# DeltaNet scan: a triangular inverse that begins in packed 32x32 blocks and is joined twice, with decay masks and output sums on other engines

## What is computed

```python
decay = exp(where(incl, g_cum[:, None] - g_cum[None, :], -inf))
a_mat = where(strict, (beta * k) @ k.T * decay, 0)
wu    = solve_triangular(a_mat + eye, [beta*k*exp(g_cum), v*beta])   # per chunk
qk    = (q @ k.T) * decay
# then, chunk after chunk, with the state S (64 x 64 per head):
v_new = u - w @ S
o     = (q * exp(g_cum)) @ S + qk @ v_new
S     = S * exp(g_last) + k_tail.T @ v_new
y     = o_forward + flip(o_backward)
```

## Time and profile before

| | |
|---|---|
| median of 3 runs | 4050.82 us (4047.32 to 4050.98) |
| profiled execution, its own time | 4048.99 us |
| its span | 4047.2 us |
| mean granted TensorE clock | 0.976 |
| TensorE busy | 3825.9 us, 95% |
| VectorE, ScalarE, POOL busy | 1951.6, 1121.1, 905.1 us |

### The profile page before, as it was taken

The page is one execution under the profiler, slowest core; times in us unless marked ns, Lnnn a source line. Parts: engine busy times, 40 slices in busy tenths (PEclk is TensorE's granted clock), DMA queues, the critical chain, the costliest instruction groups (busy, mean ns, idle before and its releaser), DMA issues.

```text
span 4047.2 us, 75588 instructions
## 1 busy us (share of the span) xinstructions
PE 3825.9 (95%) x32478; PEld 3201.9 (79%) x32478; DVE 1951.6 (48%) x3457; ACT 1121.1 (28%) x2430; POOL 905.1 (22%) x659
## 2 busy tenths in 40 slices
PE   6999999899899999999998999999899899999997
PEld 5668888788787888888886668878788778888886
DVE  3455566444456333333357464565444564333446
ACT  3444242333413111111114452252333321000111
POOL 1000100122103333333322001100222034443442
PEclk8999999899899999999998999999999899999999
DMA  4230000100000101101111120001000101111111
GB/s 179 102 149 32 22 22 22 61 3 3 23 32 32 42 31 41 42 31 41 41 40 73 63 105 22 22 12 42 32 3 3 43 32 53 42 52 52 41 52 52
DMA packets 30518, 180.81 MB, mean 45 GB/s; under 512 B 2592, under 2 KB 7968, under 8 KB 15136
## 3 DMA queue, kind: packets, MB, share of 16 engines
q1 hardware_dynamic: 28944, 173.66, 11.7%
q10 hardware_dynamic: 1296, 3.07, 0.2%
HBM read 168.32 MB, written 8.39 MB: 44 GB/s over the span
## 4 chain that ended last, share of the span: by engine, by line
PE 85%; DVE 8%; ACT 4%; issue 2%; DMA 1%; POOL 1%; ACTq 0%; POOLq 0%; DVEq 0%; SPq 0%
PE ps L1364 37%; PE ps L768 9%; PE ps L778 8%; PE ps L803 4%; PE ps L901 3%; PE ps L1228 3%; PE ps L1236 2%; PE ps L1239 2%; PE ps L943 2%; PE ps L986 1%; PE ps L1317 1%; PE ps L1207 1%; PE ps L812 1%; PE ps L1291 1%; PE ps L1008 1%
## 5 line engine op out<-in xcount | busy, mean ns | idle before, releaser
L1364 PE MATMUL ps<-Yn_parts,ring_parts 128*128 128x512 f32 (+1 forms) x3888 | 798.9, 367 | 2.4 <-DVE Yn_parts L2610 2.1
L1364 PEld LDWEIGHTS ps<-Yn_parts,ring_parts 128*128 128x128 f32 x3888 | 671.2, 189 | 126.7 <-DVE Yn_parts L2610 5.4
L1364 PE MATMUL ps<-temp_parts,ring_parts 128*128 128x512 f32 (+1 forms) x2560 | 726.5, 369 | 5.0 <-DVE Hn_parts L2551 3.6
L2871 POOL TENSOR_TENSOR ring_parts<-ring,consts 128x2048 fp32r<-128x2048 f32 x62 | 286.5, 4621 | 1187.4 <-DMA ring<-in_ff 1187.4
L1364 PEld LDWEIGHTS ps<-temp_parts,ring_parts 128*128 128x128 f32 x2560 | 464.9, 189 | 88.0 <-DVE Hn_parts L2551 4.1
L768 PE MATMUL ps<-ring_parts,Xn_parts 128*128 128x256 f32 x2560 | 506.1, 293 | 24.1 <-DVE Hn_parts L2122 16.2
L2498 DVE SCALAR_TENSOR_TENSOR Xn<-ps,mods,Xn 128x256 f32<-128x256 f32 (+1 forms) x364 | 251.7, 692 | 574.2 <-PE ps L1364 504.3
L1364 PE MATMUL ps<-Hn_parts,ring_parts 128*128 128x512 f32 (+1 forms) x1280 | 471.4, 368 | 0.0
L768 PEld LDWEIGHTS ps<-ring_parts,Xn_parts 128*128 128x128 f32 x2560 | 418.4, 196 | 27.3 <-issue 22.6
L1926 ACT ACTIVATE Yn<-ps 128x256 f32<-128x256 f32 (+1 forms) x160 | 88.6, 554 | 1237.6 <-PE ps L1364 1237.6
L2609 DVE TENSOR_TENSOR Yn<-Yn 128x256 f32<-128x256 f32 (+1 forms) x160 | 191.3, 1196 | 402.7 <-ACT Yn_parts L1928 402.7
(11 more groups left out here) (318 smaller groups left out, 5610.1 us busy)
## 6 DMA issues: line engine op xcount, KB each, us to landing
ring<-in_ff SPq DMA_DIRECT2D x64, 1024.0 KB, 4.7
ring<-in_ada SPq DMA_DIRECT2D x22, 2048.0 KB, 9.0
ring<-in_halves SPq DMA_DIRECT2D x28, 1024.0 KB, 4.8
Xn<-in_x SPq DMA_DIRECT2D x1, 5120.0 KB, 16.8
Hn<-in_ada SPq DMA_DIRECT2D x2, 2048.0 KB, 21.1
Xn<-in_x SPq DMA_DIRECT2D x2, 2048.0 KB, 18.5
kept_x<-Xn SPq DMA_DIRECT2D x4, 1024.0 KB, 4.5
Xn<-kept_x SPq DMA_DIRECT2D x1, 4096.0 KB, 15.5
```

Source lines behind the costliest of these rows:

```text
L1364: m = pe.matmul(ps[:, bank, 0:hi - lo], w[a][:, k, j * P:(j + 1) * P], x[b][:, k, lo:hi], start=(k == 0 and part == 0), stop=(k == k_n - 1 ...
L2871: link(TT(by(half_hi[s]), by(half[s]), spread(ones, 1, HALF // P), ALU.mult))
```

## The change

The levels stop at 32x32 blocks, of which four lie side by side on the diagonal, so that each matmul of `seed`, `y` and `u` is 32x32 and there are 16 of them per head group where there were 8; the tables, `first`, `lower`, `upper` and `step` are 32 wide. There are four levels in place of five. Two new operations join pairs of 32-blocks to 64: `a` and `b`; `x` and `z` join these to 128 as before. VectorE spreads the last level's blocks with a mask (`in_pair`, `in_four`) into `half` and `inv`, which also writes the zeros that memsets wrote before. `arg` goes from VectorE to ScalarE (a ReLU of the negated difference, with `exp` of its negative), the triangle mask becomes a multiplication on POOL (`mask`), `at` and `qkd` become two operations, and the sum into `d_o` goes from VectorE to POOL (`acc`). The plan is rewritten. The core of the diff:

```diff
@@ scan_plan
-            for what in ("gsum", "arg", "exp", "gram", "at", "first"):
+            for what in ("gsum", "arg", "exp", "mask", "gram", "at", "qkd", "first"):
                 plan += both(what, 0)
-            plan += one("gsum", 1, 0) + both("seed", 0)
+            for what in ("gsum", "arg", "exp", "mask"):
+                plan += one(what, 1, 0)
+            plan += both("seed", 0)
...
-                plan += late("w", 0) + y(1) + late("w", 1) + late("kept", 0) + late("kept", 1) + soon("arg", 0)
-                plan += late("v", 0) + soon("exp", 0) + u(1) + y(2) + late("o", 0) + both("keg", s_) + soon("gram", 0)
-                plan += u(2) + late("out", 0) + soon("at", 0) + late("v", 1) + y(3) + soon("gsum", 1)
-                plan += u(3) + soon("first", 0) + soon("arg", 1) + y(4) + soon("exp", 1) + late("o", 1) + soon("gram", 1)
-                plan += u(4) + late("out", 1) + soon("at", 1) + y(5) + soon("first", 1) + u(5) + both("kt", s_)
-                plan += then("gsum", 0) + soon("seed", 0) + [("x", s_, 0, 0)] + soon("seed", 1) + [("z", s_, 0, 0)]
+                plan += late("w", 0) + y(1) + late("w", 1) + late("kept", 0) + late("kept", 1)
+                plan += u(1) + late("v", 0) + soon("gram", 0) + soon("at", 0)
+                plan += y(2) + late("v", 1) + late("o", 0)
+                plan += u(2) + late("out", 0) + late("o", 1) + soon("qkd", 0) + soon("first", 0)
+                plan += y(3) + soon("gsum", 1) + late("out", 1)
+                plan += u(3) + soon("arg", 1) + soon("exp", 1) + soon("mask", 1) + late("acc", 0)
+                plan += y(4) + soon("gram", 1) + both("keg", s_)
+                plan += u(4) + [("a", s_, 0, 0)] + soon("at", 1) + late("acc", 1)
+                plan += [("b", s_, 0, 0)] + soon("qkd", 1) + soon("first", 1) + then("gsum", 0)
+                plan += [("x", s_, 0, 0)] + soon("seed", 0) + both("kt", s_) + then("arg", 0) + then("exp", 0) + then("mask", 0)
+                plan += [("z", s_, 0, 0)] + soon("seed", 1)
@@ TensorE
-                            for r in blocks:
-                                m = pe.matmul(prod[r, of(h)], at_[r, h, r], b["lower"][r, h, :], start=True, stop=True, skip_group_check=True)
+                            for r in blocks32:
+                                m = pe.matmul(prod[r, of32(h)], at_[r, h, r], b["lower"][r, h, :], start=True, stop=True, skip_group_check=True)
...
+                    if what == "a":
+                        for q_ in range(2):
+                            pe.wait_ge(sems[f"u_wide{q_}"], nth(f"u_wide{q_}", 2 * s_ + 1))
+                            for h in range(H):
+                                for c in range(2):
+                                    have, off = (blocks32[n_] for n_ in pair_of(q_, c))
+                                    m = pe.matmul(ps[off, 2 + q_, of32(h)], sc[q_]["at"][now][have, h, off],
+                                                  sc[q_]["half"][have, h, 32 * q_:32 * q_ + 32],
+                                                  start=True, stop=True, skip_group_check=True)
...
+                    if what == "b":
+                        for q_ in range(2):
+                            pe.wait_ge(sems[f"u_far{q_}"], nth(f"u_far{q_}", 2 * s_ + 1))
+                            pe.wait_ge(sems[f"u_wide{q_}"], nth(f"u_wide{q_}", 2 * s_ + 2))
...
+                            for h in range(H):
+                                m = pe.matmul(ps[off, 2 + q_, 256 + 32 * h:288 + 32 * h], full[off, h, off], step[off, h, :],
+                                              start=True, stop=True, skip_group_check=True)
+                            m.then_inc(sems[f"u_lmm{q_}"], tally(f"u_lmm{q_}"))
+                            for h in range(H):
+                                for c in range(2):
...
@@ ScalarE
+                    if what == "arg":
+                        act.wait_ge(sems[f"u_g{q}"], nth(f"u_g{q}", s_ + 1))
...
+                            m = A(b["ex"][:, h, :], rows_, ACT.Relu, bias=g_tok[:, h, at_col:at_col + 1], scale=-1.0)
+                        ln.link(m)
...
+                        A(flat(b["ex"]), flat(b["ex"]), ACT.Exp, scale=-1.0).then_inc(sems[f"u_decay{q}"], tally(f"u_decay{q}"))
@@ VectorE
-                            m = STT(b["ex"][:, h, :], rows_, g_tok[:, h, at_col:at_col + 1], upto[:, q, :], ALU.subtract, ALU.min)
...
+                    if what == "u" and lv == 4:
+                        dve.wait_ge(sems[f"u_umm{q}"], nth(f"u_umm{q}", 5 * s_ + 5))
+                        TT(b["half"].rearrange("p h (n c) -> p h n c", n=2), spread(hd(ps[:, q, 0:P]), 2, 2), spread(in_pair, 1, H), ALU.mult)\
...
+                    if what == "a":
...
+                            TT(sc[q_]["inv"][now].rearrange("p h (n c) -> p h n c", n=4), spread(hd(ps[:, q_, P:2 * P]), 2, 4), spread(in_four, 1, H), ALU.mult)\
...
-                        link(TT(flat(b["o"]), tail[:, 256:512], flat(b["o"]), ALU.add))
-                        link(TT(d_o[:, tile, :], d_o[:, tile, :], flat(b["o"]), ALU.add))
-                        dve.sem_inc(sems[f"u_done{q}"], tally(f"u_done{q}"))
+                        TT(flat(b["o"]), tail[:, 256:512], flat(b["o"]), ALU.add).then_inc(sems[f"u_done{q}"], tally(f"u_done{q}"))
@@ POOL
+                    if what == "mask":
+                        pool.wait_ge(sems[f"u_decay{q}"], nth(f"u_decay{q}", 2 * s_ + 2))
+                        TT(b["ex"], b["ex"], spread(tri[:, q, :], 1, H), ALU.mult).then_inc(sems[f"u_staged{q}"], tally(f"u_staged{q}"))
...
+                        link(pool.drain())
+                        for r in blocks32:
                             link(TT(b["first"][r], b["at"][now][r, :, r], spread(levels[r, q, 0, :], 1, H), ALU.mult))
...
+                    if what == "acc":
+                        pool.wait_ge(sems[f"u_done{q}"], nth(f"u_done{q}", s_ + 1))
+                        link(TT(d_o[:, tile, :], d_o[:, tile, :], b["o"].rearrange("p h c -> p (h c)"), ALU.add))
```

More of the change, by code:

```diff
@@ L401, in build @@
             b = {}
-            for n_ in ("lower", "upper", "step", "first"):
-                b[n_], r0_ = cut(ringf, r0_, H, 64)
+            for n_ in ("lower", "upper", "first"):
+                b[n_], r0_ = cut(ringf, r0_, H, 32)
+            b["step"], _ = cut(ringf, r0_, H, 32)
+            b["far"], r0_ = cut(ringf, r0_, H, 64)
+            b["half"], r0_ = cut(ringf, r0_, H, 64)
             for n_ in ("at", "qkd", "inv"):
@@ L1256, in dn_scan @@
+                            pe.wait_ge(sems[f"u_inv{q_}"], nth(f"u_inv{q_}", 3 * s_ + 2))
                         for h in range(H):
                             for q_ in range(2):
-                                have, off = blocks[q_], blocks[1 - q_]
-                                m = pe.matmul(ps[have, 2 + q_, of(h)], sc[q_]["step"][off, h, :], sc[q_]["inv"][now][off, h, off],
+                                have, off = blocks64[q_], blocks64[1 - q_]
+                                m = pe.matmul(ps[have, 2 + q_, of(h)], sc[q_]["far"][off, h, :], sc[q_]["inv"][now][off, h, off],
@@ L2444, in dn_scan @@
+                        m.then_inc(sems[f"u_kq{q}"], tally(f"u_kq{q}"))
+                    if what == "qkd":
                         if s_ >= 2:
                             dve.wait_ge(sems[f"u_omm{q}"], nth(f"u_omm{q}", s_ - 1))
-                            dve.wait_ge(sems[f"u_xmm{q}"], nth(f"u_xmm{q}", s_ - 1))
-                        for h in range(H):
-                            STT(at_[:, h, :], gram[:, h % 2, 1, h // 2, :], d_bt[:, tile, 4 * q + h:4 * q + h + 1], b["ex"][:, h, :],
-                                ALU.mult, ALU.mult)
```

203 lines of the change are left out of this document (114 added, 89 removed).

## The result

The changed kernel takes **4144.8 us** (median of 4 runs, 4142.9 to 4160.0) against 4050.9 of the kernel before: a ratio of 1.024, 95% interval 1.022 to 1.027. It is slower by 94 us where 90 us less were forecast, far outside the range. The profiled execution took 4142.9 us.

The account below looks back on a forecast made before the run. TensorE's issue order was taken as the bound; -7.9 levels, -0.8 seeds, +1.5 joins, +0.6 tile shape changes, +2.1 waits make -4.5 us a step, -90 us over 10 steps and 2 layers: 3961 us, range 3925 to 4025.

Parts of the forecast that it names:

- The price of a group: Level products: a round of four 32x32 tiles takes 31.7 ns, so `y` takes 0.254 us and `u` 0.507.
- The work of the other engines: VectorE loses work, POOL gains to 11.6 us a step, ScalarE about 9; beyond the counted waits it costs nothing.
- The sum for a TensorE that gets its instructions at full clock: One scan step: all terms together give -4.5 us, from 31.0 to 26.5.
- One sign: Steady scan: TensorE busy 80 to 87% if the forecast is right.
- Rivals 3 and 4: Level groups: a round takes 45 to 58 ns (4009 to 4057, chance 0.14), or each record 29.2 ns (4289, 0.08).
- the first term: Levels of a step: 10 `y` and 10 `u` become 8 and 8, 14.0 us becomes 6.1, -7.9.
- Waits: TensorE's waits in a step: 3.6 us in place of 1.5, +2.1.
- 1.7 idle: Ahead of `gsum`: VectorE needs 3.4 us after the last `u`, TensorE has only `a` and `b`, 1.7 us.
- `gram` of direction 1 ... 0.6: In the levels: `gram` of direction 1 waits 0.6 us for `arg` behind four level copies.
- 1.0 idle: End of a step: ScalarE needs 3.1 us for copies, `arg` and `exp`; TensorE has 2.0 of work, idle 1.0.
- Rival 5: Steady scan: TensorE's clock falls to 1.2 GHz in one stretch a step, about 2 us each, 4000 us; chance 0.08.

Follow-up runs that it names:

- e1: The changed kernel with level products issued for only the first and third 32x32 block of each head, half the level instructions: 4059.8 us, ratio 1.002.
- e13: e9 with `gram` of direction 1 issued after the last `u` instead of ahead of it: 4066.6 us, ratio 1.002.
- e11: The kernel before with only `y`'s products split in two by weight columns, a third of e3's added instructions: 4049.7 us, ratio 1.000.
- e3: The kernel before with every level product issued as two of half the weights' columns, same arithmetic, twice the level instructions: 4161.9 us, ratio 1.028.
- e10: The kernel before with ScalarE's two copies ahead of `z` made three times each, lengthening TensorE's wait there: 4115.9 us, ratio 1.016.
- e16: e10 with only the first 32 of 64 moving columns in every level product: 4436.1 us, ratio 1.094.
- e9: e1 with `gsum` of the tile after next issued after `z` instead of ahead of `x`: 4020.8 us, ratio 0.994.
- e15: The kernel before with only the first 32 of 64 moving columns in every level product: 4051.1 us, ratio 1.000.

## Why the prediction was wrong

**What was right.** *The price of a group*: 32 records of 32x32 follow each other 0.25 us apart (0.25 to 0.27 at full clock in the trace; 16 in 0.25 us in e1). The row that it was worked out from the earlier trace rows stands at a granted clock of 0.58 and not at half, so that it came out so exactly is in part luck. *The work of the other engines*: busy shares fell on VectorE and ScalarE, and POOL is named in no wait of TensorE or VectorE in 780 to 1050 (once for each of them nearer the scan's ends). *The sum for a TensorE that gets its instructions at full clock*: forecast 26.5 us a step; e13's undisturbed steps are mostly 25.5 to 26.3, e1's 27.6 to 28.0. Both are kernels that leave half of the level products out, and e13 has another order, so they bear on the sum of the terms and not on the change. One sign came true by luck: TensorE was to be busy for 80 to 87% of the steady scan, and is for 82% (229.79 of 280 us), of steps 8 us longer than meant. Rivals 3 and 4 are refuted as what they were, a price of each record inside its group: records of 32x32 with their loads come at about 8 ns each there. The Trainium skill, "TensorE: Matmul & The Clock Gate", section "Wait — 56ns, not 53.3ns?", with its least interval of 25 ns, thus holds at most for matmuls that meet on one tile: four side by side go below it, as the trace shows.

**The step that failed** is the first term, "10 `y` and 10 `u` become 8 and 8 ... -7.9", and with it the list of the terms. It priced what the array does with 24 groups, and put at nothing, without a reason, that a packed group takes in 64 instructions in 0.25 us. Of rival 3, "packing helps half", the direction was right (the weight loads and records do count), but it put the limit into every record, with 11 to 14.6 ns each; rival 4's 29.2 ns "in a long run" was near the true rate, but it was charged to every group. The runs show a limit on *blocks*: 256 instructions come no sooner than about 3.3 us after the last 256, and mostly 3.5 to 3.9 where TensorE stands for them, or 26 to 30 ns a record with its load. The kernel before takes 0.467 us for 16 records and their loads, 3.7 us for a block of nothing but level groups, by chance just above 3.3 (e11 shows no loss, e3 4.4 us a step). The changed one asks for 2170 instructions in a step instead of 1350, in bursts: 31 us of stops in 270 us, 4 us a step, plus what the clock makes of them. The forecast's step couldn't be had at all: 2170 instructions are 8.5 blocks, at 3.3 us each 28 us a step even if they were used evenly (an estimate from these numbers), against 26.5. The Trainium skill does have the mechanism: "Runtime: NRT & Kernel Launch", section "Instruction fetch mechanics", says that each engine's instructions stream in 16 KiB blocks of 256 while the current one executes. But it calls the crossing mostly hidden, since dispatch is slower than the fill. For TensorE with packed fp32 tiles the traces show the opposite.

**Waits.** "1.7 idle" ahead of `gsum` is one stretch of 3.3 us (975.4 to 978.8) with nothing but the joins' small products in it, of which TensorE stands idle for 0.7; "`gram` of direction 1 ... 0.6" is 0.7 (2.7 us in 4 times), and "1.0 idle" at the end of a step is 0.6 ahead of `w` (4.2 us in 7 times, put down to "issue"). The term was too long rather than too short: 3.6 us a step forecast, some 1.8 in the changed kernel (14 us in 270) and 2.5 in e1 (22 us). What it left out is what such a stretch sets off.

**Rival 5, the clock**, had the mechanism ("if one stretch in each step went to 1.2 GHz") and was given 0.08 and 2 us a step. The forecast's reason against it, that the clock stays 1.00 beside waits of 0.8 us, is the second step that failed: the changed kernel shows 0.80 in mid-scan. e10 shows that a wait of 2.4 us sets it off, at a price of 1.5 us where 64 columns move; e1's bad steps cost 6.5 us, e13's 12.7, e16's 21. The rows before the change, with a full clock beside waits of 0.8 us, came from products with 64 moving columns; the change halves them.

**What stays open.** The slowdown isn't split to the microsecond. With its late instructions alone the kernel would probably lose about what e3 does, which no run shows; how much of 34.6 us a step is stop and how much half clock can't be read off one run, since the clock falls at the stops, and a TensorE at half clock also asks for its instructions more slowly. Nor was it settled why the clock comes back where it does in e1 and e13 (in the stretch of `x`, seeds, `z` and `gsum`). No kernel was tried that packs as the change does with fewer instructions; e9, which leaves half of them out, is 30 us faster than before at best, and is no proof that one exists.

## To carry over

Before packing small tiles, count the instructions, weight loads included, and ask in how few microseconds 256 of them are used up: in this kernel level groups at 3.7 us cost nothing, at 2.8 us between longer operations nothing either, and at 1.8 us they cost 14% of a step. Look for "issue" inside a group of equal products, and for the instruction queue's packets. And don't price a wait by its length where TensorE's clock is full only because it never waited long: a wait of 2.4 us cost 1.5 us more with 64 moving columns and 21 us more with 32.

## What was unexpected of the hardware

- The instruction supply of TensorE: 16.4 KB blocks never less than 3.25 us apart and 3.5 to 4 in the DMA view where it stops, while the queue is busy for 0.5% of the span; and every longer stop inside a level group a multiple of 256 instructions from the others of its scan, in the changed kernel as in e3.
- A TensorE that is busy for 48.00 of 48.00 us and stays at half clock (e16, products with 32 moving columns), and that holds full clock on the same products where it never waited long (e15).
- A round of tiles at full clock takes the same time with 64 weight columns and 32 moving as with 32 and 64 (groups of 16 records 0.47 and 0.45 us), and about half with 32 of both (0.25): the longer of the two sides sets it.
